# A fused two-block kernel on one core: the first products on TensorE in another order, with a narrower gate product

## The reference, cut to what matters

```python
def rmsnorm(x, g):
    xf = x.astype(jnp.float32)
    y = xf * lax.rsqrt(jnp.mean(xf * xf, axis=-1, keepdims=True) + EPS)
    return (y * g.astype(jnp.float32)).astype(x.dtype)
...
h = rmsnorm(x, norm_g[i])
proj = h @ fox_w_in[j]
q, k, v, f_logit, q_mem, z = split_cols(
    proj, [MAIN_W, MAIN_W, MAIN_W, N_MAIN_HEADS, MEM_W, INNER])
main = fox_attention(q, k, v, f_logit, fox_b_f[j])
...
log_f = jax.nn.log_sigmoid(f_logit.astype(jnp.float32) + b_f.astype(jnp.float32))
c = jnp.cumsum(log_f, axis=1).transpose(0, 2, 1)
...
memo = mem_cross_attention(q_mem, mem_n, w_mem_kv[i])
```

## Time and profile before

| what | value |
|---|---|
| median of 3 runs | 1591.98 us (1591.89 to 1592.17) |
| the profiled execution, its own time | 1591.62 us |
| its span in the trace | 1589.8 us |
| PE busy | 1581.5 us, 99% of the span |
| PEld busy | 1361.7 us, 86% |
| DVE busy | 998.0 us, 63% |
| ACT busy | 724.6 us, 46% |
| POOL busy | 602.9 us, 38% |
| DMA, mean | 115 GB/s; 315 GB/s in the first 24.3 us |

### The profile page before, as it was taken

One profiled execution on the slowest core, in us unless ns is written; L12 is line 12 of the kernel. 1 busy time (PEld: TensorE's weight loads), 2 busy tenths in 40 slices (PEclk: granted clock), 3 DMA queues, 4 the chain that ended last, 5 costly groups with the idle time before them and its releaser, 6 DMA issues.

```text
span 1589.8 us, 21815 instructions
## 1 busy us (share of the span) xinstructions
PE 1581.5 (99%) x8856; PEld 1361.7 (86%) x8856; DVE 998.0 (63%) x1477; ACT 724.6 (46%) x1114; POOL 602.9 (38%) x301
## 2 busy tenths in 40 slices
PE   9999999999999999999999999999999999999998
PEld 7888898889888888888888778888888889999997
DVE  7888867676766365455553776782356785555554
ACT  6533443343432344455555454324434545545454
POOL 1002113221245334355556333353223335555552
PEclk9999999999999999999999999999999999999999
DMA  6554434344466413333333332132112233232321
GB/s 245 172 173 147 143 117 140 112 133 126 127 216 210 156 66 112 101 106 101 102 104 137 121 125 66 53 107 83 41 54 67 80 106 107 93 107 94 106 93 54
DMA packets 54413, 182.95 MB, mean 115 GB/s; under 512 B 6556, under 2 KB 7196, under 8 KB 53928
## 3 DMA queue, kind: packets, MB, share of 16 engines
q1 hardware_dynamic: 54024, 181.02, 34.7%
q10 hardware_dynamic: 288, 0.52, 0.1%
HBM read 174.42 MB, written 3.96 MB: 112 GB/s over the span
## 4 chain that ended last, share of the span: by engine, by line
PE 95%; DVE 3%; ACT 0%; issue 0%; POOL 0%; DVEq 0%
PE banks L470 93%; PE banks L473 2%; DVE ada L1235 1%; DVE WA L1235 0%; DVE TM L1860 0%; DVE wl L1266 0%; ACT Sc L2207 0%; DVE TM L1870 0%; DVE nmx L1338 0%; POOL wl L2877 0%; DVE Sc L1348 0%; DVE Y L1860 0%; DVE Y L1849 0%; DVE T L1235 0%; POOL Y L2969 0%
## 5 line engine op out<-in xcount | busy, mean ns | idle before, releaser
L2877 POOL TENSOR_TENSOR wl<-raw,wh 128x1024 fp32r<-128x1024 f32 x139 | 346.4, 2495 | 386.0 <-ACT wh L2210 386.0
L470 PE MATMUL banks<-HH,wh 128*128 128x512 f32 (+2 forms) x944 | 362.0, 386 | 0.3 <-DVE X L1543 0.3
L470 PE MATMUL banks<-HL,wh 128*128 128x512 f32 (+2 forms) x944 | 352.4, 379 | 0.0
L2210 ACT ACTIVATE wh<-raw 128x1024 fp32r<-128x1024 f32 x246 | 257.3, 1051 | 193.7 <-PE banks L470 190.2
L470 PE MATMUL banks<-HH,wl 128*128 128x512 f32 (+1 forms) x936 | 251.2, 380 | 0.1
L470 PEld LDWEIGHTS banks<-HH,wh 128*128 128x128 f32 (+1 forms) x944 | 177.2, 188 | 36.9 <-issue 2.6
L470 PEld LDWEIGHTS banks<-HL,wh 128*128 128x128 f32 (+1 forms) x944 | 177.1, 188 | 33.7 <-issue 1.2
L470 PEld LDWEIGHTS banks<-HH,wl 128*128 128x128 f32 x936 | 172.1, 188 | 35.2 <-issue 1.5
L470 PE MATMUL banks<-wh,HH 128*128 128x256 f32 x448 | 127.8, 285 | 0.0
L470 PE MATMUL banks<-wl,HH 128*128 128x256 f32 x448 | 126.7, 283 | 0.0
L470 PE MATMUL banks<-wh,HL 128*128 128x256 f32 x448 | 126.7, 283 | 0.0
(11 more groups left out here) (433 smaller groups left out, 3267.4 us busy)
## 6 DMA issues: line engine op xcount, KB each, us to landing
raw<-wst_dram SPq DMA_DIRECT2D x294, 512.0 KB, 3.4
X<-xT_dram SPq DMA_DIRECT2D x8, 512.0 KB, 5.9
CB<-sums_dram SPq DMA_DIRECT2D x12, 256.0 KB, 3.2
D<-dec_dram SPq DMA_DIRECT2D x12, 256.0 KB, 2.8
x_dram<-X SPq DMA_DIRECT2D x3, 512.0 KB, 6.3
QS<-QX SPq DMA_DIRECT2D x24, 64.0 KB, 2.8
KSw<-KX SPq DMA_DIRECT2D x24, 64.0 KB, 2.0
X<-x_dram SPq DMA_DIRECT2D x3, 512.0 KB, 5.3
```

Of the source, the lines that this page charges most:

```text
L470: return pe.eng.matmul(dst, w, x, start=start, stop=stop, skip_group_check=True)
L2210: return eng.activation(dst, src, ACT.Copy)
L2877: tt(wl[:, q, :], raw[:, i % NRAW, :], wh[:, q, :].bitcast(F32), ALU.subtract).then_inc(*by_pool("low", u))
```

## The change

The gate columns are handled as a later tile of the same kind ("g") already was. The low parts of the 32 gate columns are written by DVE not into a `wl` tile of their own but into columns 32 to 63 of the same blocks of `wh`. One matmul with all 128 columns then gives high*high on rows 0 to 31 of PSUM bank 4 and low*high on rows 32 to 63; a second with 32 columns adds high*low on rows 0 to 31. That is two matmuls for each k, not three. The sum of rows 0 to 11 and 32 to 43 still has to be made: SP moves rows 32 to 43 of `CT` down to partitions 0 to 11 (`CT_LOW`) with a DMA, and DVE adds them.

The order of the first products is written out by hand: gates for k = 0 to 3, then u1's 24 matmuls in three parts (high weights with `HH`, low weights with `HH`, high weights with `HL`), with the gates' high products for k = 4 to 7 among them and their low ones last. On ACT and DVE the split of u1 stands between the fourth and the fifth slice of x, not behind the eighth.

```diff
+    CT_LOW = at("CT_LOW", [12, T], C0 + 26)
...
-        slot_128("forget", feed.take(), HH, HL, T, 4, lambda k: done("h", "x0", k), lambda k: done("l", "x0", k))
-        by_pe.also("w free", 0)
-        unit_f(("qm", 0))
+        first, second = feed.take(), feed.take()
+        gate_w, q_w = halves_of(first, 8)[0], halves_of(second, 4)
+
+        def gates_high(k):
+            pe.wait_ge(done("high", first), done("low", first), done("h", "x0", k))
+            mm(bank[4], gate_w[:, k, :], HH[:, k, :], k == 0, False)
+
+        def gates_low(k):
+            pe.wait_ge(done("l", "x0", k))
+            mm(bank[4][0:32, :], gate_w[:, k, 0:32], HL[:, k, :], False, k == 7).then_inc(*by_pe("unit", "forget", 0))
+
+        def first_q(k, part):
+            for nt in range(2):
+                c = slice(128 * nt, 128 * nt + 128)
+                pe.wait_ge(done("h", "x0", k), (done("high", second), done("low", second), done("l", "x0", k))[part])
+                mm(bank[nt], q_w[part % 2][:, k, c], (HL if part == 2 else HH)[:, k, :], k == 0 and part == 0, False)
+
+        for k in range(4):
+            gates_high(k)
+            gates_low(k)
+        for k in range(4):
+            first_q(k, 0)
+        for k in range(4):
+            gates_high(4 + k)
+            first_q(k, 1)
+        for k in range(4):
+            first_q(k, 2)
+        for k in range(4, 8):
+            gates_low(k)
+        by_pe.also("w free", first)
+        by_pe.also("w free", second)
+        free[4] = (done("kept", "forget", 0),)
+        features(("qm", 0), HH, HL, range(4, 8), False, True, (0, 1), feed.take(), kh=1)
...
+            elif PLAN[i][0] == "f":
+                w = gate_columns(u)
+                dve.wait_ge(done("high", u))
+                tt(w[:, :, 32:64], gate_rows(i), w[:, :, 0:32].bitcast(F32), ALU.subtract).then_inc(*by_dve("low", u))
+                by_dve.also("raw free", i)
...
         for k in range(8):
+            if k == 4:
+                feed.split_next()
             scaled_low("x0", k, X, P("g0", k), HH, HL)
         dve.wait_ge(done("consts"))
         eng.tensor_copy(onesr[:, :], onesf[:, :]).then_inc(*by_dve("ones"))
-        feed.split_next()
         feed.take()
...
-        feed.unit()
         dve.wait_ge(done("unit", "forget", 0), done("scale", "x0"))
         tt(CT[:, :], bank[4], R[:, :], ALU.mult).then_inc(*by_dve("kept", "forget", 0))
+        feed.unit()
+        dve.wait_ge(done("logits low"), done("kept", "forget", 0))
+        tt(CT[0:12, :], CT[0:12, :], CT_LOW[:, :], ALU.add).then_inc(*by_dve("logits"))
...
         for k in range(8):
+            if k == 4:
+                feed.split_next()
             scaled_high("x0", k, X, P("g0", k), HH, done("x in", k // 2), done("par"))
-        feed.split_next()
...
-        act.wait_ge(done("kept", "forget", 0))
+        act.wait_ge(done("logits"))
...
-        units(12)
+        units(2)
+        sp.wait_ge(done("kept", "forget", 0))
+        dma(CT_LOW[:, :], CT[32:44, :]).then_inc(*low_in("logits low"))
+        units(10)
```

More of the change, by code:

```diff
@@ L284, in build @@
         signal(n + "_in", 16) for n in ("cst", "rot", "filter", "del", "dft", "cx", "gk", "masks", "idft", "cb"))
-    rows_in, stored, stored_too = signal("rows_in", 16), signal("stored", 16), signal("stored_too", 16)
+    low_in, rows_in, stored, stored_too = signal("low_in", 16), signal("rows_in", 16), signal("stored", 16), signal("stored_too", 16)
     x_out = [signal("x_out%d" % i, 16) for i in range(4)]
@@ L568, in unit_t, with slot_gates @@
                     beside()
[L570 to L582, removed]
+        def slot_gates(tag, u, xh, xl, n, b, hi=nothing, lo=nothing, width=64):
             w = halves_of(u, 8)[0]
@@ L587, in slot_gates @@
                 pe.wait_ge(hi(k), *free[b])
-                mm(bank[b][0:64, 0:n], w[:, k, 0:64], xh[:, k, 0:n], k == 0, False)
+                mm(bank[b][0:width, 0:n], w[:, k, 0:width], xh[:, k, 0:n], k == 0, False)
                 pe.wait_ge(lo(k))
```

## The result

| | median | runs | range |
|---|---|---|---|
| before | 1591.98 us | 19 | 1591.63 to 1592.73 |
| after | 1594.36 us | 19 | 1594.09 to 1595.84 |

The ratio is 1.0016, with a 95% interval of 1.001 to 1.0022: slower by some 2.4 us, within the range that was given (forecast 1594.6). The profiled execution of the changed kernel took 1594.51 us, its span is 1592.7.

A forecast was written before the change was run, and what follows sets the result against it. DVE, taking turns with ACT, was taken to bound the first 94.66 us. DVE's 2.0 delay plus 0.65 for the logits, 2.65 on 1591.62, gave 1594.3; with 0.36 for the median, 1594.6 us (8 in 10: 1593.1 to 1595.8).

The forecast's parts named there:

- What bounds the start: Up to 94.66 us DVE, taking turns with ACT, sets the time; PE carries it only from there.
- ACT ahead of slices 4 to 7: Behind slice 3 ACT idles 2.5 us for u1's load; DVE's squares' copy, at 15.70 before, comes 2.0 us later.
- The logits: Low logits' DMA (2.0 us, hidden behind u7 and u8) and DVE's 0.68 addition make ACT start 0.65 us later.
- Eight matmuls count for nothing: The gates' 24 products become 16, 1.8 us of PE work where DVE sets the time; counted at nothing.
- PE, 1.0 later from its idle stretch: PE idles about 2.4 us until u1's `wh` at 12.51 and reaches the first key product at 25.3, not 24.34.
- The forecast wait for u3's low part, 27.4: At u3's low products PE waits for DVE and takes that `wl` at 27.4, 2.0 later than 25.41.
- the fall of the clock: Rival: PE's clock halves for 5.9 us behind the idle stretch ending near 12.5, giving 1595.4; chance 0.13.
- The rival's 0.8 beyond DVE's shift: With PE's clock halved, second gate product and scores near 50 us wait for PE: 2.65 + 0.8 = 3.5.
- its own 3.7: With PE's clock halved, PE reaches u3's low products 3.7 us behind the kernel before.
- "0.6 us to spare" ahead of 94.66: PE's 0.61 us idle wait for DVE's `wl` before 94.66 was read as PE arriving with time to spare.
- "wrong if the wait at 97.3 is gone": Sign: no PE wait for `wl` before the values' products near 97.3 would mean PE, not DVE, decides there.
- The sum: PE's start of the values' products moves by 2.0 + 0.65 = 2.65, from 94.66 to 97.3.

The follow-up runs named there:

- zero products: Changed kernel plus 11 products of zeros on TensorE in the gap behind the gates of slices 0 to 3; 1594.57 us.
- u1 early: Changed kernel with u1's load issued ahead of the third and fourth piece of x on SP's queue; 1591.87 us.
- narrow only: Kernel before with only the narrow gate product (16 matmuls, not 24) in the old order, low logits moved by DMA and added on DVE; 1592.67 us.
- zero products, split back: Changed kernel with 11 products of zeros in TensorE's gap and u1's split on ACT and DVE behind the eighth slice again; 1593.00 us.
- split back: Changed kernel with u1's split on ACT and DVE behind the eighth slice of x again, TensorE keeping its new order; 1594.62 us.
- no move: Changed kernel without the DMA of the low logits and DVE's addition, leaving the low weights' product out of the result; 1594.54 us.
- before, copies on ACT: Kernel before with two copies of bank 7 (second half of the memory attention's turned probabilities) moved from DVE to ACT; 1591.53 us.
- after, copies on ACT: Changed kernel with two copies of bank 7 (second half of the memory attention's turned probabilities) moved from DVE to ACT; 1594.24 us.

## Why the prediction was right, point by point

*What bounds the start.* Right in what it led to, too simple as a statement. The prediction has DVE set the time for all of the first 94.66 us, from a chain that it shows from 60.8 on the earlier trace rows. Over the first 60 us the chain of the kernel before is PE's, without a break:

```profile
1.25 58.88 PE banks L470 x330
```

PE and DVE take two paths that end within hundredths of each other. One length shows it across kernels, from DVE's clamp of the logits (line 1407 before) to the start of the `wl` pair that PE waits for near 95 us:

| kernel (profiled run) | clamp | wl | between |
|---|---|---|---|
| before | 41.53 | 93.30 | 51.77 |
| after | 44.27 | 96.03 | 51.76 |
| zero products | 44.73 | 96.46 | 51.73 |
| u1 early | 41.83 | 93.57 | 51.74 |
| narrow only | 42.54 | 94.27 | 51.73 |
| zero products, split back (PE late, clock kept) | 42.54 | 94.68 | 52.14 |
| split back (slow clock) | 44.30 | 97.17 | 52.87 |
| no move (slow clock) | 44.02 | 97.21 | 53.19 |
| before, copies on ACT | 41.84 | 93.28 | 51.44 |
| after, copies on ACT (clock kept) | 44.25 | 95.08 | 50.83 |

In the first five rows the length is the same within 0.04, whether PE comes early or not: DVE's work sets it, and taking eight products off PE gains nothing. Where PE is late with its query product, it is longer. Taking 1.2 us off DVE shortens it by 0.33 in the kernel before, where PE has no more lead than that.

So each of two delays was enough for the whole loss: DVE's (zero products, 1594.57) and PE's on the slow clock (split back, 1594.62). Only with both gone is the kernel near the one before (1593.00, and 1591.87 with u1 loaded early). The forecast counted DVE's alone. That it also holds in the runs in which the clock fell is luck: PE was then late by as much.

*ACT ahead of slices 4 to 7.* Forecast: idle 2.5, DVE 2.0 later. Measured: 2.62 and 2.10; u1 took 8.1 us to land in this run, 7.8 in the earlier trace rows. Right. The early load, which takes the loss back, and the split put back with the clock kept (1.6 us) show it to be the cause.

*The logits.* Forecast +0.65, measured 0.64 in the trace, and with the clock kept 0.60 between two traces and 0.75 between two medians. Right. The DMA was hidden; what it costs is the addition, 0.68 us on 12 partitions (which are an eleventh of the 128, not the sixteenth that the prediction has).

*Eight matmuls count for nothing.* Right, though the place where they are lost was named wrong (DVE's `HL`, not u3's low part first).

*PE, 1.0 later from its idle stretch.* Too little, even where the clock is kept: the keys, at 24.34 before, begin at 25.64 in the changed kernel with the copies on ACT and at 25.92 with the zero products and the split back. PE starts again at 12.76 and not 12.55, and its step is 0.230 us (12.88 us for 56 products). Where the clock fell it was more, 27.27 in the changed kernel and 28.42 with the split back. The forecast wait for u3's low part, 27.4, came where the clock was kept (27.51 with the copies on ACT) and not in the changed kernel's own trace. I had priced the fall of the clock as a rival at 0.13: the fall itself came in 14 of 19 runs (those with a mean clock under 1.000), a price in time in 4, at 1595.36 to 1595.84 where 1595.4 was forecast. The rival's 0.8 beyond DVE's shift was not worked out: its own 3.7 less 2.65 is 1.05. The "0.6 us to spare" ahead of 94.66 was the wrong step: it is a wait behind DVE work that itself waits for PE, not slack, so the experiments that leaned on it (split back, no move, the copies in the changed kernel) came out with less than I expected. The wait is 0.60 or 0.61 with PE late or level and 0.94 with PE early, so the sign "wrong if the wait at 97.3 is gone" could not tell the two apart. In the prediction it did no harm to the forecast, since DVE was late by as much as PE.

*The sum.* 2.65 was forecast for the start at 94.66, and 2.73 measured. The medians moved by 2.38; the profiled execution of before was 0.36 faster than its median, and that of after 0.15 slower than its own, so a few tenths lie in which execution was profiled.

## What to carry to other kernels

Where the trace's longest-busy engine has even a short wait that comes back in the same place, ask whose chain ends there: here work taken off the busy engine ahead of that point was worth nothing. Work taken off the other was worth something only as far as the busy one had a lead (1.2 us off DVE gave 0.33). Read the chain of waits from the start of the stretch, and remember that it names one path: where two are level, undo each by itself and then both. Before an instruction is moved up in an engine's order, look up when its transfer lands: an engine that works in order stops for all that stands behind it, and here one load issued two places earlier took back the loss. A wait is slack only if nothing in front of it waits for the waiting engine.

## What the runs showed of the hardware that I had not expected

- Behind an idle stretch of TensorE of 2.43 us the granted clock fell to half in the profiled execution, and by the mean clocks in most runs of the changed kernel but not in all: five of the 19 kept 1.000. With the split back (2.33 us idle, 0.83 granted already within the stretch, then 0.50) the same stretch cost more. The Trainium skill, "TensorE: Matmul & The Clock Gate", section "Why this matters for your kernels", warns of such gaps only where they are longer than this one; the measurement decides. Filling the gap with products of zeros kept the clock at 1.00 in the stretches behind it.
- The granted clock of the profile doesn't show the slow start. In the kernel before it reads 1.00 from 0 to 7 us, where the weight loads lie 0.43 us apart; the level there is read from the spacing.
- An addition on 12 partitions (12x512) took 0.68 us, the same as 128x512.
- The issue of the DMA of 12 rows held SP for 0.88 us, where the median of the 294 loads of 512 KB is 0.33 (the longest 0.82):

```profile
40.59 0.88 SPq L3095 DMA_DIRECT2D CT_LOW<-CT  x1
```

- It was back by 42.80 at the latest, 2.2 us after its issue.
